# Expert rows written per token into two DRAM tables, with their weights looked up by slot

## The reference, cut to what matters

```
expert_id, weight = top-1 group of 4, then top-2 of 8 experts in it      # two experts per token
f[t] = sum over the two experts e of token t:
       weight[t,e] * (silu(h[t] @ w_gate[e]) * (h[t] @ w_up[e])) @ w_down[e]     # 32 experts, 1024 -> 512 -> 1024
x  = LN(alpha * x + gate2 * f) * ln2_g + ln2_b
```

## Time and profile before

| | us |
|---|---|
| median of 3 runs | 973.48 (972.28 to 974.92) |
| the profiled execution's own time | 973.71 |
| its span, first to last instruction | 971.8 |
| PE busy | 914.9 (94%) |
| DVE busy | 381.5 |
| ACT busy | 244.5 |
| POOL busy | 114.0 |

### The profile page before, as it was taken

One profiled execution on the slowest core, in us unless ns is written; L12 is line 12 of the kernel. 1 busy time (PEld: TensorE's weight loads), 2 busy tenths in 40 slices (PEclk: granted clock), 3 DMA queues, 4 the chain that ended last, 5 costly groups with the idle time before them and its releaser, 6 DMA issues.

```text
span 971.8 us, 11764 instructions
## 1 busy us (share of the span) xinstructions
PE 914.9 (94%) x4253; PEld 540.5 (56%) x4253; DVE 381.5 (39%) x662; ACT 244.5 (25%) x356; POOL 114.0 (12%) x173
## 2 busy tenths in 40 slices
PE   3789999999999999999999999998988999999994
PEld 2457776888888888786444344434443444444331
DVE  4522434456344236798532232222222222232235
ACT  2422233442233235445411011101100110111024
POOL 2210257100001000000000000000000000000031
PEclk9889999999999999999999999999999999999998
DMA  9984763346455822908999999999999899999973
GB/s 369 340 270 169 258 218 131 129 173 256 176 195 169 221 86 87 301 2 349 375 405 427 428 429 426 427 427 431 424 428 427 332 427 426 430 426 430 423 293 114
DMA packets 46634, 297.72 MB, mean 306 GB/s; under 512 B 4418, under 2 KB 6562, under 8 KB 30946
## 3 DMA queue, kind: packets, MB, share of 16 engines
q1 hardware_dynamic: 36352, 263.99, 67.1%
q0 software_dynamic: 9600, 31.18, 9.6%
q10 hardware_dynamic: 610, 1.66, 0.5%
HBM read 275.81 MB, written 21.00 MB: 305 GB/s over the span
## 4 chain that ended last, share of the span: by engine, by line
PE 84%; ACT 3%; DMA 3%; issue 3%; DVE 3%; SPq 2%; POOL 0%; DVEq 0%; POOLq 0%; ACTq 0%
PE bank L600 81%; DMA modraw<-in_w_mod 2%; PE bank L870 2%; SPq L381 2%; ACT x_rows L1073 2%; DMA y_first<-round_y,pos_y 1%; DVE wo_lo L1642 0%; PE bank L657 0%; DMA round_y<-yout 0%; ACT w_hi L1073 0%; POOL y_second L588 0%; POOL y_first L588 0%; DVE yout L1933 0%; DVE g_a L1659 0%; DVE res L1702 0%
## 5 line engine op out<-in xcount | busy, mean ns | idle before, releaser
L600 PE MATMUL bank<-up_w,x_t 128*64 128x512 f32 x512 | 225.0, 592 | 0.0
L600 PE MATMUL bank<-gate_w,x_t 128*64 128x512 f32 x512 | 225.0, 592 | 0.0
L600 PEld LDWEIGHTS bank<-gate_w,x_t 128*64 128x64 f32 x512 | 70.1, 137 | 143.1 <-issue 143.1
L600 PE MATMUL bank<-h_hi,w_hi 128*128 128x512 f32 x320 | 126.5, 395 | 1.6 <-ACT h_hi L1107 1.6
L600 PE MATMUL bank<-h_hi,w_lo 128*128 128x512 f32 x320 | 126.1, 394 | 0.0
L600 PE MATMUL bank<-down_w,hid_t 128*64 128x512 f32 x512 | 118.8, 606 | 7.6 <-issue 6.6
L600 PE MATMUL bank<-h_lo,w_hi 128*128 128x512 f32 x320 | 125.3, 399 | 0.0
L1306 ACT ACTIVATE sg_hid<-bank 64x512 f32<-64x512 f32 x33 | 19.5, 592 | 350.0 <-PE bank L600 350.0
L1915 DVE TENSOR_TENSOR sg_hid<-bank,sg_hid 64x512 f32<-64x512 f32 x32 | 22.2, 694 | 204.4 <-ACT sg_hid L1306 204.3
L1477 DVE TENSOR_TENSOR w_lo<-raw,w_hi 128x1024 fp32r<-128x1024 f32 x56 | 68.6, 1227 | 77.8 <-ACT w_hi L1073 77.8
L600 PEld LDWEIGHTS bank<-h_lo,w_hi 128*128 128x128 f32 x320 | 60.5, 189 | 25.3 <-issue 11.7
(11 more groups left out here) (315 smaller groups left out, 1119.4 us busy)
## 6 DMA issues: line engine op xcount, KB each, us to landing
down_w<-in_w_exp_down SPq DMA_DIRECT2D x32, 2048.0 KB, 18.1
gate_w<-in_w_exp_gate SPq DMA_DIRECT2D x31, 2048.0 KB, 16.4
up_w<-in_w_exp_up SPq DMA_DIRECT2D x31, 2048.0 KB, 20.9
modraw<-in_w_mod SPq DMA_DIRECT2D x24, 1024.0 KB, 8.8
raw<-in_w_in SPq DMA_DIRECT2D x9, 2048.0 KB, 9.8
round_y<-zrow POOLq DMA_DIRECT2D x6, 2048.0 KB, 7.7
raw<-in_w_branch_b SPq DMA_DIRECT2D x2, 2048.0 KB, 9.4
raw<-in_w_branch_a SPq DMA_DIRECT2D x2, 2048.0 KB, 10.9
```

The source lines that it names most:

```text
L600: return pe.matmul(out, lhsT, rhs, start=start, stop=stop, skip_group_check=True)
```

## The change

Each token gets two rows in a DRAM tensor `chosen_y`: row t for its first expert, row 512 + t for its second. An expert's results are stored there at once, already times the token's weight.

- For that, a slot must know its token and its weight. DVE computes for each assignment the two values (row, weight) in `vals` and the place rank x 32 + expert in `pos_y`. POOL writes the pairs of 8 bytes to a DRAM table `slot_table` with eight indirect DMAs, waits for all of them, and reads the first 64 ranks of every expert back as `slotw`, once for each half of the partitions. DVE makes `slot_row` from it, and `sides` multiplies the weight into the factor of `gate_rows`. In expert 0, `sides`, `gate_rows` and `out_rows` now wait for `slotw`, and stand behind the lower halves `h2_lo`.
- The two stores of 32 or 64 rows become one indirect DMA with all 128 partitions of 2 KB. A slot without a token has a row number past the table's end, which the DMA drops (`bounds_check`). `few`, `w_last`, `scaling` and `is_last` go, and the zeroes shrink from six DMAs of 2048 KB to 4096 KB and 128 KB.
- Experts 30 and 31 are both kept out of DRAM, and come in by `near_rows` on PE from `yout[0]` and `yout[1]`.
- After the stores of experts 0 to 29, SP reads the tables with eight plain loads of 512 KB, tiles 2, 3, 0, 1. POOL adds the two rows of a tile (`total` + `y_out`), and DVE adds the residual (`with_residual`). For tiles 2, 3 and 0 that stands in DVE's order ahead of `out_rows` of expert 31.
- ACT issues the loads of `ln2_g` and `ln2_b` (512 KB each) in expert 30 and no longer in 31. `centred_gain(3)` now stands ahead of `gain(1)`.

The core of the diff:

```diff
@@ SP, after the last weights
+            for s in range(3):
+                sp.wait_ge(y_st[s], 16 * 10)
+                sp.sem_inc(sp_go, 1)
+            sp.wait_ge(x_st, 16 * allx + 16)
+            for i in (2, 3, 0, 1):
+                for j, rows in enumerate((total[i], y_out[i])):
+                    sp.dma_start(rows[:, :], chosen_y[TOK * j + 128 * i:TOK * j + 128 * i + 128, :]).then_inc(f_g[i], 16)
@@ POOL
-            for k in range(LAST_ROW // 512):
-                pool.wait_ge(pe_blk, 22 + 3 * k)
-                pool.dma_start(round_y[512 * k:512 * k + 512, :]..., zeroes).then_inc(s_zero, 16)
+            pool.dma_start(chosen_y[:, :]..., zeroes).then_inc(s_zero, 16)
+            pool.dma_start(slot_table[:, :]..., zrow[0:64, :]).then_inc(s_zero, 16)
...
+            pool.wait_ge(dve_pos, 1)
+            for j in range(2):
+                for i in range(TILES):
+                    pool.indirect_dma_start(slot_table[:, :], bass.IndirectOffsetOnAxis(pos_y[:, j, i:i + 1], 0), vals[:, j, i, :], None,
+                                            bounds_check=TOK * NEXP - 1, oob_is_err=False).then_inc(s_table, 16)
+            pool.wait_ge(s_table, 16 * 2 * TILES)
+            for c in range(2):
+                pool.dma_start(slotw[CAP * c:CAP * c + CAP, :, :], by_slot[0:CAP, :, :]).then_inc(s_slotw, 16)
-                pool.dma_start(round_y[bass.ds(row, rows), 0:512], y[0:rows, :]).then_inc(done, 16)
-                pool.dma_start(round_y[bass.ds(row, rows), 512:1024], y[64:64 + rows, :]).then_inc(done, 16)
+            def store(rows, y, done):
+                pool.indirect_dma_start(chosen_halves, bass.IndirectOffsetOnAxis(rows, 0), y, None,
+                                        bounds_check=4 * TOK - 1, oob_is_err=False).then_inc(done, 16)
-            for i in range(TILES):
-                for j, y in enumerate((y_second, y_first)):
-                    pool.indirect_dma_start(y[i][:, :], None, round_y[0:LAST_ROW, :], ...).then_inc(f_g[i], 16)
+            for n, i in enumerate((2, 3, 0, 1)):
+                pool.wait_ge(f_g[i], 32)
+                pool.tensor_tensor(total[i][:, :], total[i][:, :], y_out[i][:, :], ALU.add).then_inc(pool_j, 1)
@@ PE, expert 30 and 31, and the end
+                if e >= NEXP - 2:
+                    pe.wait_ge(dve_sel, j + 1)
+                    (four transposes of sel to B[2])
+                    if j == 0:
+                        mm(B[7][:, :], ident, cst[:, 0:512])
+            near_rows(0, 2)
+            near_rows(1, 0).then_inc(f_z, 1)
+            near_rows(1, 1).then_inc(f_z, 1)
             for i in (2, 3):
-                (residual, two products with scaling for y_first, two for y_second, last_rows(i))
+                pe.wait_ge(f_b, i - 1)
+                for c in range(2):
+                    mm(sums[i][c][:, :], ident, total[i][:, 512 * c:512 * c + 512], start=(i == 3), stop=False)
+                if i == 3:
+                    near_rows(0, 3, start=False)
+                near_rows(1, i).then_inc(f_z, 1)
@@ DVE
+            def with_residual(n, i):
+                dve.wait_ge(pool_j, n + 1)
+                dve.tensor_tensor(total[i][:, :], total[i][:, :], res[:, i, :], ALU.add).then_inc(f_b, 1)
@@ expert(0)
-                    sides(e)
-                    gate_rows(e)
                     (columns_in, next_pair, h2_lo)
+                    dve.wait_ge(s_slotw, 32)
+                    ch.did(dve.tensor_scalar(slot_row[:, :], slotw[:, :, 0], half_row[:, 0:1], None, ALU.add))
+                    sides(e)
+                    gate_rows(e)
                     out_rows(e)
@@ the last expert
                     gate_rows(e)
+                    if e == NEXP - 1:
+                        for n, i in enumerate((2, 3, 0)):
+                            with_residual(n, i)
                     out_rows(e)
@@ summed(i)
+                dve.wait_ge(f_b, i + 3)
@@ the end
-            joined(0)
+            with_residual(3, 1)
             summed(0)
-            joined(1)
             summed(1)
             inverses()
             centred_gain(2)
             gain(0)
             inverse(2)
             scaled_bias(2)
+            centred_gain(3)
             gain(1)
-            centred_gain(3)
             inverse(3)
             scaled_bias(3)
```

More of the change, by code:

```diff
@@ L576, in _ @@
[L576 to L585, removed]
-            for i in range(TILES):
-                for j, y in enumerate((y_second, y_first)):
-                    pool.indirect_dma_start(y[i][:, :], None, round_y[0:LAST_ROW, :],
-                                            bass.IndirectOffsetOnAxis(pos_y[:, 1 - j, i:i + 1], 0),
-                                            bounds_check=LAST_ROW - 1, oob_is_err=False).then_inc(f_g[i], 16)
+            pool.wait_ge(dve_pos, 1)
@@ new lines, in further_store, with expert @@
+            def further_store(turns):
+                pool.wait_ge(x_sem["yo"], turns + 2)
+                pool.sem_inc(pool_go, 1)
+                store(slot_row_x[:, 0:1], yout_x[:, :], x_st)
+                pool.wait_ge(x_st, turns * 16 + 32)
+                pool.sem_inc(pool_go, 1)
+            def expert(e):
+                more = pool.value_load(tab[0:1, 0, bass.ds(e, 1)], min_val=0, max_val=7)
+                with pool.If(more > 0):
+                    further_table(e, CAP)
+                if e < NEXP - 2:
+                    pool.wait_ge(m_sem["yo"], e + 1)
+                    store(slot_row[:, e:e + 1], yout[e % 3][:, :], y_st[e % 3])
+                with pool.If(more > 0):
+                    first = pool.value_load(tab[0:1, 1, bass.ds(e, 1)], min_val=0, max_val=FURTHER)
+                    further_store(first)
+                    with pool.If(more > 1):
+                        with pool.Fori(1, more) as r:
+                            further_table(e, pool.snap((r + 1) * CAP))
+                            further_store(pool.snap(first + r))
@@ L591, in _ @@
+            for e in range(NEXP):
+                expert(e)
+            for n, i in enumerate((2, 3, 0, 1)):
+                pool.wait_ge(f_g[i], 32)
+                pool.tensor_tensor(total[i][:, :], total[i][:, :], y_out[i][:, :], ALU.add).then_inc(pool_j, 1)
             pool.wait_ge(s_ln2, 32)
```

229 lines of the change are left out of this document (104 added, 125 removed).

## The result

| | before | changed |
|---|---|---|
| median (range), us | 975.01 (972.28 to 978.62) | 981.18 (978.75 to 984.15) |
| profiled execution: time, span, mean granted clock | 973.71, 971.8, 0.985 | 981.18, 979.5, 0.977 |

The ratio of changed to before is 1.0056, with a 95% interval of 1.0031 to 1.0080: slower by 0.56%, 5.5 us. (The ratio is taken over all executions; the two medians alone differ by 6.2.) The forecast was 973.8 us with a range of 966.5 to 983, so the time lies in the range. It lies outside the forecast's own likeliest case (969.5 to 978), and only the two slower rivals had carried the range so far.

A forecast was written before the change was run, and what follows sets the result against it. DMA bytes were taken to set the pace up to about 740 us, and work after the gathers the tail. Terms -2.6 + 0.1 + 0.3 + 2.5 = +0.3 on 973.5 gave 973.8 us, range 966.5 to 983.

The forecast's parts named there:

- likeliest case: Whole kernel: the summed terms hold, 973.8 us, own range 969.5 to 978, chance 46%.
- dropped rows that cost their time: Rival at each of the 30 stores: dropped rows cost as much as written ones, +9.1 us, 982.6; chance 17%.
- late table: Rival at expert 1: the slot table lands 5.6 us late, which counts in full, 979 us; chance 13%.
- Store bytes: 504 to 737 us: 1.02 MB less stored, DMA arrives earlier and PE takes all of it, -2.6 us.
- Table's round trip: Scatter and reload of the slot table before `hidden` of expert 1: 1.1 us to spare, +0.3 us charged.
- forecast's own sign of being wrong: At expert 1: `hidden` starting after 491 us on the old scale.
- Routing: Six small DVE operations ahead of the wait for the logits, mostly in idle time: +0.1 us, at most 1.2.
- POOL and DVE in turns: Tail: POOL's joins and DVE's two-input operations exclude each other; `out_rows` of expert 31 at 948.9 instead of 941.1.
- joins don't hold DVE up: Rival in the tail: `out_rows` of expert 31 at 943.0, in all -6.3 us, 967.2; chance 24%.
- Tail: From the last experts to the end: later `out_rows`, sums and last SP issue, end at 974.3, +2.5 us.
- clock charge of 1 us: Tail: PE's pause from about 942 to 949 lowers its granted clock, charged 1 us.

The follow-up runs named there:

- early_hidden_keep: early_hidden with the extra TensorE product of keep_clock added: 969.27 us, ratio to before 0.9943.
- early_hidden: joins_reordered with DVE's `hidden(1)` ahead of the wait for `slotw` when expert 0 has no further round: 969.76 us, ratio to before 0.9952.
- all_rows_stored: Changed kernel with slots without a token also storing their row, each to a spare place: 983.36 us, ratio to before 1.0074.
- shift128: Changed kernel with 127 unreached copies and the branch ahead of expert 19's further block in DVE's program: 980.26 us, ratio to before 1.0053.
- keep_clock: Changed kernel with one useless TensorE product between the counting products and expert 0's selection: 979.67 us, ratio to before 1.0053.
- joins_on_vector: Changed kernel with the four joins of chosen rows on DVE instead of POOL: 972.34 us, ratio to before 0.9971.
- joins_reordered: joins_on_vector with tiles in order 0 to 3 and most adds behind `out_rows` of expert 31: 970.86 us, ratio to before 0.9954.
- three shifted kernels: Changed kernel with 4, 63 or 127 unreached copies ahead of expert 19's further block in DVE's program: 975.39, 977.87, 980.26 us.
- shift64: Changed kernel with 63 unreached copies and the branch ahead of expert 19's further block in DVE's program: 977.87 us, ratio to before 1.0027.

## Why the prediction was right or wrong

The number fell in the range by luck. Above 978 the range belonged to two rivals, dropped rows that cost their time (982.6) and a late table (979), and neither is what made the kernel slower.

- **What is missing, and made most of the difference:** the code of the further round. The chain of before showed DVE waiting 5.63 us for it; the prediction only said that the further round starts there, and didn't ask where the block would lie once the change lengthens DVE's program. It costs about 3.7 us, and no step, bound or rival held it. The diff doesn't show it, since the place comes from the whole length of the code ahead.
- **Store bytes, -2.6.** Right in DMA's time, and too large in PE's. POOL's queue moved 1.23 MB less in 504 to 737 us (I had 1.02), and the weights' queue 1.13 MB more, 2.6 us at 427 GB/s. But PE's waits fell from 6.6 to 5.56 us, not to 4. One reason is ahead of that stage: from 440 to 504 us the weights' queue had moved 23.87 MB instead of 24.59, while SP's request came late (DMA share 0.21 in 472 to 476, 0.64 before). It isn't the only one: early_hidden_keep lacks that delay (24.81 MB), and there A less routing is 273.3, only 1.3 us less than before. So the term is about -1.2 by early_hidden and early_hidden_keep, each one execution and hardly clear of noise, and where the rest goes stays open. Added bytes cost 3.1 to 4.2 us per MB.
- **Dropped rows** (rival, 17%): wrong, by all_rows_stored. The bound was taken from the right side.
- **Table's round trip, +0.3.** The steps were right (`slotw` forecast for 486.9, measured 486.9 to 488.8 at full clock; the eighth scatter for 472.8, measured 472.95), but the 1.1 us to spare were used up. (The quiet landing in the earlier trace rows is 2.48 us, which I read as 2.4; it changes nothing.) Where the clock stayed up, `hidden(1)` started at 491.3 to 492.4, the forecast's own sign of being wrong, and PE lost 1.5 to 1.7 us there (shift128, keep_clock, joins_on_vector). At A some 0.8 to 1.1 us of it are left by A less routing of shift128 and keep_clock (274.2, 274.5) against 273.4 of the two kernels with an early `hidden(1)`, again near the noise. The rival "table late" had the place, with a price of 5.6 us, over three times too high.
- **Routing, +0.1.** Not seen: `slot_of` starts at 459.1 and 459.6, and between executions of one code it moves by more.
- **POOL and DVE in turns.** Right in size: `out_rows(31)` came 7.1 us later from B, forecast 7.8. joins_on_vector shows the mechanism, and with joins_reordered it splits the 7.1: the turns are 3.5 us of it (13.46 against 9.96), and the adds that merely stand ahead of `out_rows` are 3.2 (9.96 against 6.74). The rival that joins don't hold DVE up is wrong.
- **Tail, +2.5.** 2.3 in the profile; B to end is 39.9 to 40.1 in the three shifted kernels and keep_clock too. Inside it, the second sum 3.2 later (forecast 4.4), ACT's last sum +1.1 (2.6), SP's last issue +3.9 (5.3), and less given back at the end than I took. The clock charge of 1 us: granted clock 0.73 in 956 to 960.

In sum the forecast's +0.3 becomes -1.2 + 1.0 + 3.7 + 2.3 = +5.8, against 5.5 measured. The last two terms carry it. The first two are small beside the spread at A, so that the sum comes so near is partly chance.

## What to carry to other kernels

Where a program branches to code that it reaches only there, look for "issue" behind the branch on each engine, and treat any edit that lengthens that engine's program as one that may add or remove a whole fetch (here a wait of 5 us on DVE, some 4 on TensorE); a few unreached instructions test it in one run. An addition of two SBUF inputs that is given to GpSimd "to relieve" VectorE is only free while VectorE isn't in such operations itself. And read a margin of about a microsecond in an execution with the clock up, since a slow stretch elsewhere can empty the queue on which it hangs.

## What the runs showed of the hardware

- A branch to code further on cost 5.5 to 6.1 us on DVE in all thirteen profiled executions, under a DMA load of 414 to 431 GB/s. A second wait of 4.9 to 5.1 us, one or two instructions in, came in three of them. In all thirteen q14 brought two 8 KB packets 5.1 to 5.6 us apart, and whether the second was waited for is the difference.
- The last of the eight scatters landed 6.8 to 7.4 us after its issue while other traffic filled the queues (the four traces that show it). In shift64, with a DMA share of 0.12 in 472 to 476 us, it landed after 2.15.
- Indirect stores took DMA time by the rows that they wrote: in 504 to 737 us 1.85 MB and 2.1% where the rows without a token were dropped, 4.20 MB and 4.4% where every row was written (all_rows_stored).
- The granted clock at 460 us fell to 0.50 to 0.62 in four profiled executions of thirteen and not in the others, in one case (shift64 and shift128) with the same TensorE program.
